# Block products for more k groups in both feed-forward matrices of a decoder layer, and the activation sums, splits and transposes around them put at other places

## The reference, cut to what matters

```python
h = rms_norm(x, ffn_pre_gain[l])
gt, up = jnp.split(h @ w_ffn_in[l], 2, axis=-1)          # 2048 x 2*5632
x = x + rms_norm((jax.nn.silu(gt) * up) @ w_ffn_out[l],  # 5632 x 2048
                 ffn_post_gain[l])
```

## Time and profile before

| | |
|---|---|
| median of 3 runs | 1490.3 us (1489.94 to 1490.7) |
| the profiled execution | 1490.09 us, of which the span from first to last instruction is 1488.4 us |
| TensorE busy | 1477.6 us, 99% of the span |
| VectorE busy | 1122.2 us, 75% |
| ScalarE busy | 855.6 us, 57% |
| DMA | 305 MB, mean 205 GB/s |
| feed-forward input, from its first late unit to the end | 820.88 to 1249.44 us |
| feed-forward output, first and second half | 1249.44 to 1365.09, 1365.09 to about 1480 us |

### The profile page before, as it was taken

The page is one execution under the profiler, slowest core; times in us unless marked ns, Lnnn a source line. Parts: engine busy times, 40 slices in busy tenths (PEclk is TensorE's granted clock), DMA queues, the critical chain, the costliest instruction groups (busy, mean ns, idle before and its releaser), DMA issues.

```text
span 1488.4 us, 19388 instructions
## 1 busy us (share of the span) xinstructions
PE 1477.6 (99%) x6694; PEld 1216.7 (82%) x6694; DVE 1122.2 (75%) x1317; ACT 855.6 (57%) x1045; POOL 151.4 (10%) x286
## 2 busy tenths in 40 slices
PE   9999999999999999999999999999999999999997
PEld 7888887888888888888888888888888888888876
DVE  6878988855554587657476878988888876887897
ACT  7645455565666544656678556666656654554653
POOL 0000000050220000000000102222220221200000
PEclk9999999999999999999999999999999999999999
DMA  9755555665565655966555576574756656556545
GB/s 341 238 187 177 182 176 190 187 210 186 187 196 171 238 185 178 333 195 212 170 184 184 185 262 211 165 259 159 256 188 213 216 191 242 185 185 224 195 159 198
DMA packets 89859, 305.08 MB, mean 205 GB/s; under 512 B 13056, under 2 KB 13568, under 8 KB 88768
## 3 DMA queue, kind: packets, MB, share of 16 engines
q1 hardware_dynamic: 80144, 285.12, 57.4%
q0 software_dynamic: 9216, 18.63, 3.8%
q10 hardware_dynamic: 432, 0.45, 0.1%
HBM read 294.19 MB, written 2.10 MB: 199 GB/s over the span
## 4 chain that ended last, share of the span: by engine, by line
PE 97%; DVE 2%; DMA 0%; issue 0%; ACT 0%; DVEq 0%; ACTq 0%
PE acc L1894 10%; PE acc L1896 10%; PE acc L1895 10%; PE side L2201 5%; PE side L2200 5%; PE side L2199 5%; PE side L1894 3%; PE side L1896 3%; PE side L1895 3%; PE acc L2201 3%; PE acc L2200 3%; PE acc L2199 3%; PE tr L1896 3%; PE tr L1894 3%; PE tr L1895 3%; PE tr L2199 2%
## 5 line engine op out<-in xcount | busy, mean ns | idle before, releaser
L634 ACT ACTIVATE w_hi<-raw 128x1024 fp32r<-128x1024 f32 x312 | 329.8, 1061 | 266.1 <-PE side L2201 110.9
L1128 DVE TENSOR_TENSOR w_lo<-raw,w_hi 128x1024 fp32r<-128x1024 f32 x324 | 390.9, 1222 | 116.1 <-ACT w_hi L634 105.4
L1123 DVE TENSOR_TENSOR w_lo<-raw,w_hi 128x1024 fp32r<-128x1024 f32 x262 | 320.9, 1227 | 201.5 <-ACT w_hi L616 197.1
L616 ACT ACTIVATE w_hi<-raw 128x1024 fp32r<-128x1024 f32 x262 | 276.9, 1059 | 281.2 <-PE acc L1896 165.7
L1894 PE MATMUL acc<-w_hi,xT_hi 128*128 128x512 f32 x504 | 198.3, 394 | 0.1
L1896 PE MATMUL acc<-w_hi,xT_lo 128*128 128x512 f32 x504 | 196.3, 389 | 0.0
L1895 PE MATMUL acc<-w_lo,xT_hi 128*128 128x512 f32 x504 | 196.3, 389 | 0.0
L589 POOL DMA_DIRECT2D hT_st<-h_blk x176 | 93.5, 540 | 499.1 <-DVE h_blk L1175 470.4
L1894 PEld LDWEIGHTS acc<-w_hi,xT_hi 128*128 128x128 f32 x504 | 94.6, 188 | 22.2 <-issue 2.2
L1896 PEld LDWEIGHTS acc<-w_hi,xT_lo 128*128 128x128 f32 x504 | 94.6, 188 | 20.0
L1895 PEld LDWEIGHTS acc<-w_lo,xT_hi 128*128 128x128 f32 x504 | 94.7, 188 | 19.1
(11 more groups left out here) (482 smaller groups left out, 2870.4 us busy)
## 6 DMA issues: line engine op xcount, KB each, us to landing
raw<-in_units SPq DMA_DIRECT2D x530, 512.0 KB, 4.1
hT_st<-h_blk POOLq DMA_DIRECT2D x176, 32.0 KB, 2.7
x_tok<-in_x SPq DMA_DIRECT2D x4, 512.0 KB, 5.6
qkT<-qk_blk POOLq DMA_DIRECT2D x64, 32.0 KB, 3.2
xres<-in_x POOLq DMA_DIRECT2D x1, 2048.0 KB, 10.7
m_raw<-in_mem_t POOLq DMA_DIRECT2D x1, 2048.0 KB, 8.5
mq<-in_mem POOLq DMA_DIRECT2D x1, 2048.0 KB, 15.3
x_raw<-in_x_t SPq DMA_DIRECT2D x6, 256.0 KB, 6.1
```

The source lines that it names most:

```text
L616: a_.activation(w_hi[:, j % RING], raw[:, j % RING], ACT.Copy).then_inc(hi_ready, 1)
L634: a_.activation(w_hi[:, v % RING], late_raw[slot], ACT.Copy).then_inc(hi_ready, 1)
L1123: v_.tensor_tensor(w_lo[:, s], raw[:, s], w_hi[:, s].bitcast(F32), ALU.subtract).then_inc(lo_ready, 1)
L1128: v_.tensor_tensor(lo[:, v % RING], late_raw[slot], hi[:, v % RING].bitcast(F32), ALU.subtract).then_inc(lo_ready, 1)
```

## The change

`PAIRS` gets two k groups for chunk pairs 3, 5 and 7 too, where it had one. The first half of the output gets a fourth k group, and the second half takes its groups in the order 3, 1, 2, 0. There are five sets of activation sums for the output instead of four: group 0 is used in both halves, and its sums are made a second time (`SUMS[4]`), because group 3 has overwritten them. `spread` gets another lead: the first half of the output begins with eight plain units ahead of its first product instead of seven, the second with four as before. In the bodies of the input, VectorE does `hidden_product` first, `hidden_lo` three steps later and `hidden_turn` six steps later; the sums for the output groups 0 and 1 are made in the last segment of the input; and the steps of the sums, their low parts and `hidden_hi(10)`, `hidden_turn(11)`, `hidden_lo(10)` in the output are others.

```diff
-PAIRS = (0, 0, 2, 1, 2, 1, 2, 1, 2, 1, 1)
+PAIRS = (0, 0, 2, 2, 2, 2, 2, 2, 2, 1, 1)
-OUT_GROUPS = ((0, 1, 2), (0, 1, 2, 3))
-SUMS = (0, 1, 2, 3)
-SUMS_OF = ((1, 2), (3,))
+OUT_GROUPS = ((0, 1, 2, 3), (3, 1, 2, 0))
+SUMS = (0, 1, 2, 3, 0)
+SUMS_OF = ((2, 3), (4,))
@@ out_segment
-    return spread(plain, products, len(plain) - 4 - 4 * m, 6 - 2 * m)
+    return spread(plain, products, len(plain) - 4 - 4 * m, 8 - 4 * m)
@@ scalar, sums_hi and the output
-                    act.wait_ge(unit_used, OUTS[1].first + OUTS[1].order.index(("P4", 0)) + 1)
+                    act.wait_ge(unit_used, OUTS[0].first + OUTS[0].order.index(("P4", 0)) + 1)
+                if k == 4:
+                    act.wait_ge(unit_used, OUTS[1].first + OUTS[1].order.index(("P4", 3)) + 1)
-                    if v == S_FO + 2:
+                    if v == S_FO + 4:
+                        sums_hi(1)
+                    if v == S_FO + 8:
+                        act.wait_ge(hs_lo, 2)
                         hidden_hi(10)
@@ vector, the bodies of the input
                     if i > 1 and v == b.first:
-                        if i > 2:
-                            hidden_lo(i - 2)
                         hidden_product(i - 2)
+                    if i > 2 and v == b.first + 3:
+                        hidden_lo(i - 2)
-                    if i > 1 and v == b.first + (5 if i == 2 else 1):
+                    if i > 1 and v == b.first + 6:
                         hidden_turn(i - 1)
@@ vector, the last segment of the input
                 if v == BODIES[9].end + 6:
                     hidden_sums(0)
+                if v == BODIES[9].end + 9:
+                    hidden_sums(1)
@@ vector, the output
-                sums_at = {b.first + b.order.index(("P5", SUMS[k])) - 8: k for k in SUMS_OF[m]}
+                sums_at = {b.first + b.order.index(("P5", SUMS[k])) - 8: k for k in SUMS_OF[m] if m == 0}
+                los_at = {b.first + b.order.index(("P5", SUMS[k])) - 4: k for k in SUMS_OF[m]}
+                    if m == 1 and v == b.first + 10:
+                        hidden_sums(4)
-                    if v == S_FO + 3:
+                    if v == S_FO + 2:
+                        dve.wait_ge(hT_turned, 10 * 256)
+                        hidden_turn(11)
+                    if v == S_FO + 4:
                         hidden_sums_lo(0)
-                    if v == S_FO + 4:
+                    if v == S_FO + 6:
+                        hidden_sums_lo(1)
+                    if v == S_FO + 10:
                         hidden_lo(10)
-                    if v == S_FO + 6:
-                        hidden_turn(11)
-                    if v - 5 in sums_at:
-                        hidden_sums_lo(sums_at[v - 5])
+                    if v in los_at:
+                        hidden_sums_lo(los_at[v])
@@ tensor
-                        pe.wait_ge(hs_lo, g + 1)
+                        pe.wait_ge(hs_lo, 5 if (m, g) == (1, 0) else g + 1)
```

More of the change, by code:

```diff
@@ L341, in trunk @@
         e_sb = at("e_sb", 200, [NC])
-        h_f = [at(f"h_f{k}", kb, [4, SEQ]) for k, kb in enumerate((164, 48, 48, 60, 60)[:len(SUMS)])]
-        H_f = [at(f"H_f{k}", kb, [4, 2, P]) for k, kb in enumerate((120, 52, 52, 52, 52)[:len(SUMS)])]
+        h_f = [at(f"h_f{k}", kb, [4, SEQ]) for k, kb in enumerate((164, 160, 48, 48, 60)[:len(SUMS)])]
+        H_f = [at(f"H_f{k}", kb, [4, 2, P]) for k, kb in enumerate((120, 116, 52, 52, 52)[:len(SUMS)])]
         H_hi = [at(f"H_hi{k}", kb, [4, 2, P], F32R) for k, kb in enumerate((72, 168, 176))]
```

## The result

The changed kernel takes 1498.43 us, the median of 5 runs (1497.22 to 1498.94), against 1490.3: a ratio of 1.0051, with a 95% interval of 1.004 to 1.0062. It is slower by 8 us, where I had forecast 2.6. The profiled execution took 1497.22 us with a span of 1495.5, so it is 7.1 us longer in both than that of before.

The account below looks back on a forecast made before the run. TensorE was taken to set the time, with VectorE close behind at 81 to 88%. Terms -5.44 + 3.4 + 3.3 + 2.3 - 1.0 = +2.6 us gave 1492.9 us against the median 1490.3; range 1489.0 to 1497.0.

Parts of the forecast that it names:

- term (i): Output's first half: late DMAs hold ScalarE at hidden_hi(11), TensorE is 1.1 us late, lag grows to +3.3 us.
- the bodies: Input bodies 3 to 8: one wait each at the plain gate unit behind the P5s, 0.57 us a body, +3.4 us.
- The walk: Following three engine queues step by step through bodies and output to find late splits; good to some 0.15 us a body.
- The landing: GpSimd's 16 DMAs in the output's first half: last one lands 2.7 us after issue; 1.7 or 4.1 as bounds.
- Rival C: Many short waits bring TensorE's clock down; 10 us at half clock lose 5 us: 1498. Chance 0.02.
- The backlog behind P2: Output's first half: VectorE has no pause after the late split, so the lag grows from 1.1 to 3.3 us.
- The saving: Three k groups in the input and one in the output drop 24 matmuls at 0.2268 us: -5.44 us.
- Term (ii): Output's first half: sums and a low part crowd VectorE ahead of P7 of groups 2 and 3, +2.3 us.
- the second half: Output's second half: loses its old burst and wait, -1.14 with about 0.1 remaining, so -1.0 us.
- ScalarE's wait at `hidden_hi(11)`: Output's first half: ScalarE should wait some 3 us there for GpSimd's DMAs, with a split queued behind.
- B: Input bodies bound by VectorE from end to end: 1498.9 us, or 1495.9 with half of it. Chance 0.18.
- A: Gain kept, bursts covered: 1483.8 us, chance of faster 0.07; with half of the lags 1488 to 1491, chance 0.17.

Follow-up runs that it names:

- `lo1_turn8`: Changed kernel with hidden_lo one step after a body's first (was three) and hidden_turn eight (was six): 1494.96 us, ratio 1.0031.
- `out_only`: Changed kernel with the old `PAIRS`, so only the output part and the moved steps in the bodies: 1498.3 us, ratio 1.0052.
- `in_only`: Kernel before with only the input part: new `PAIRS` and the new places in the bodies: 1490.48 us, ratio 1.0002.
- `in_lo1_turn8`: Kernel before with only the input part, hidden_lo at step 1 and hidden_turn at step 8 of a body: 1487.66 us, ratio 0.9982.

## Why the prediction was wrong

The sum and its direction. Forecast +2.6 us and "same" by a narrow margin, range up to 1497.0; measured +8.1, above the range. The likeliest verdict was wrong; "slower" had 0.43.

**The step that failed is term (i)**, by its size: +3.3 us predicted, +7.1 in the trace. Of the 5.5 us by which the median lies above the forecast, 3.8 are this term, 0.4 the bodies, 0.4 small distances, and 1.0 is the further runs of after, which no trace shows. The mechanism of (i) is what the trace shows: `hidden_hi(11)` waits for the landing, P2 of group 1 is late, then a further wait. The walk up to the landing was good: it had GpSimd start at S + 8.8, and S, the start of s8, is 1249.4 plus eight plain units of 2.72, so 1271.1; it started at 1280.19, S + 9.1, because it began 0.58 us behind `hidden_lo(10)` and not 0.30. The last DMA left at 1288.16, as worked out. Then two numbers failed.

- The landing. I took 2.7 us, the median of 176 small DMAs, and their worst, 4.1, as the bound. It was 6.03 us. Those 176 were measured at the places where the kernel before issues them. The batch that the change moves was issued there from 1269.9 to 1277.9, in windows with a DMA share of 0.53 and 0.78, and landed after at most 4.0. The change moves it 10 us later, to where the share is 0.99. I named the move of ScalarE's and VectorE's steps and not what the DMA queues do at the new place. The share alone does not give the landing, though: another batch of the kernel before, at 1224.5, had the engines 0.84 busy and landed after at most 4.1. The 3.3 us more at the landing are the step from 1.1 predicted to 4.44 measured at P2. The two windows of the kernel before, and the landing of its batch there:

```profile
1270.00:1275.00 5.00, 5.00 (x24) 4.14 (x23) 4.50 (x4) 2.87 (x3) 5.00 (x10) 1.00 0.53 157
1275.00:1280.00 5.00, 5.00 (x24) 4.14 (x23) 4.28 (x5) 2.44 (x3) 3.42 (x7) 1.00 0.78 221
```
```profile
DMA to landing us min/median/max: 1.7/2.9/4.0
```

- The clock. Rival C had a chance of 0.02, and against it I held that the clock stays at 1.00 across a gap of 1.0 us. That holds, and says nothing of a gap of 4.4. The long wait was followed by half clock, which cost another 1.4 us. C's mechanism had been put at the many short waits; there it does not occur.

The backlog behind P2, which I had grow by 3.3 less 1.1, so 2.2 us up to s29, was 0.80 there (the gap from 1315.13 to 1316.09) and a fifth of a microsecond ahead of it and behind. TensorE had run six matmuls at half clock by then, which gave the splits 1.4 us to catch up. Two other traces go the same way: with 1.7 us lost to the clock (`lo1_turn8`) 0.57 us remain at s29, with 2.8 (`out_only`) nothing. No run was made to try this alone.

**What held.** The saving: 24 matmuls at 0.2268 us. The bodies: +3.4 predicted, +3.8 measured, at just the unit named, the plain gate unit behind the P5s. Here is body 3:

```profile
907.56 0.39 PE L2201 MATMUL tr<-w_hi,S_lo 128*128 128x512 f32 x1
908.23 0.50 PE L2212 MATMUL acc<-w_hi,xT_hi 128*128 128x512 f32 x1 [0.28 <-DVE w_lo L1133]
908.57 0.39 PE L2213 MATMUL acc<-w_lo,xT_hi 128*128 128x512 f32 x1
```

The distances are 0.67 and 0.34 instead of 0.2268 each, a lag of 0.44 + 0.11, and 0.08 follows elsewhere in the body. The order of VectorE ahead of it is the one that was walked (start, length, line):

```profile
902.41 1.23 DVE L1151 TENSOR_TENSOR raw<-raw,raw 128x1024 f32<-128x1024 f32 x1 [0.20 <-DVE w_lo L1133]
903.55 1.22 DVE L1133 TENSOR_TENSOR w_lo<-raw,w_hi 128x1024 fp32r<-128x1024 f32 x1
904.69 1.22 DVE L1188 TENSOR_TENSOR hT_lo<-hT_st,hT_hi 128x1024 fp32r<-128x1024 f32 x1
905.82 1.22 DVE L1151 TENSOR_TENSOR raw<-raw,raw 128x1024 f32<-128x1024 f32 x1
906.96 3.48 DVE L1133 TENSOR_TENSOR w_lo<-raw,w_hi 128x1024 fp32r<-128x1024 f32 x3
```

The starts are 1.14 us apart with `hidden_lo` (L1188) in the middle, and `lo1_turn8` took the waits away by moving that one. It moved the turn (L1180) too, but the turn stands behind the late split, at 910.36, so its place cannot have made this wait. VectorE is busy 237.01 of 248.79 us in these bodies, 95%, as said. Term (ii) held (2.3 against 2.2) and so did the second half (-1.0). ScalarE's wait at `hidden_hi(11)` was there, but 6.61 us where I had named some 3; the difference is the landing again.

**The rivals.** B, the bodies bound by VectorE, is refuted by `in_only`: one wait a body and no loss in sum. Beside it stood the Trainium skill (VectorE: DVE Perf Modes, The DRAIN you can't avoid), which has the next instruction wait until the pipe is empty, and says as well that one that is not held starts earlier. The splits' rows here are 1.22 us long and start 1.14 us apart, so the 1.22 us a split that I had worked out by it is not what they cost. A is refuted as the change stands, but half right about what is possible: with `hidden_lo` at another step the input's part does keep 2.7 us.

**What would have set the range right.** The small DMAs of the kernel before could not give the bound: their worst landing was 4.1 us in any of its windows. Its weight loads take up to 8.2 us, and a batch that is newly put beside a burst of them may take as long. With that row the term's upper end would have been some 4 us higher. The sum of the bounds was wrong besides: the upper ones make 1490.3 - 5.4 - 1.0 + 4.8 + 4.7 + 2.8 = 1496.2 and not 1498. With 4 us more they make 1500, and the measured 1498.43 lies inside.

## What to carry to other kernels

When a change moves a batch of small DMAs, read the DMA share of the window where it will land as well as the landing times of where it was: the slack of whoever waits must hold for the loaded case. An in-order engine that waits for such a batch holds up everything queued behind it (6.61 us on ScalarE became 4.44 on TensorE here), so put the waiting step where its data is sure to be there, or send sooner; each of the two took 6 us off here. And price a wait by its length: the three of 4.4 to 4.8 us cost the clock besides, 1.4 to 2.8 us, and none of up to 1.35 us did. A gain is also worth trying in parts: the input's part with `hidden_lo` and the turn moved kept 2.7 us, where the whole change lost 8.

## What the runs showed of the hardware

- 16 small DMAs of 32 KB landed after 1.7 us in the median with the DMA engines 0.45 to 0.49 busy (130 to 145 GB/s), and after 5.0 to 5.1 us, at most 6.0 to 6.4, with the engines at 0.88 to 0.99 in the window of the later ones (317 to 349 GB/s). A batch at 0.84 (276 GB/s) in the kernel before took 2.8 in the median and at most 4.1.
- Behind a gap of 4.4 us TensorE ran six matmuls at half clock, 0.43 us apart, then at full (after); behind 4.6 us thirteen (`out_only`), behind 4.8 us eight and part of a ninth (`lo1_turn8`). Gaps of up to 1.35 us left the clock at 1.00.
- The second matmul behind a wait, at full clock, starts 0.30 to 0.35 us after the first instead of 0.2268, so each wait costs 0.07 to 0.12 us over its length; in the bodies of `in_lo1_turn8`, without a wait in the list, such a distance of 0.33 to 0.34 was nearly all that remained.
